# A two-block transformer layer on one core: the last block's entry, with the gates' rows moved among the norm's tiles and the dense work of eight rounds dealt out unevenly

## The chip, the cores and the metric

The kernel runs on one core of a Trainium2 chip. TensorE (PE in the profile) multiplies matrices; VectorE (DVE), ScalarE (ACT) and GpSimd (POOL) do the rest; SyncE's queue (SP) carries the weights. Every engine works through its own list of instructions in order and waits on semaphores for the others. The metric is the time of one execution on the device in microseconds (us), lower is better.

## The reference, cut to what matters

512 tokens of 1024 channels pass a first block (banded attention, pooling, a gated feed-forward) and then a second, hybrid block. The change touches the beginning of the second block only:

```python
hn = rms_norm_2(x, w_norm)
proj = jnp.einsum("bsd,de->bse", hn, w_in.astype(f32))
q_a, k_a, v_a, z_a, b_a, a_a, q_b, k_b, v_b, z_b = jnp.split(proj, idx, axis=-1)
qkv = jax.nn.silu(causal_depthwise_conv(jnp.concatenate([q_a, k_a, v_a], -1), conv_w.astype(f32)))
...
beta = jnp.transpose(jax.nn.sigmoid(b_a), (0, 2, 1))
g = -jnp.exp(a_log.astype(f32)) * jax.nn.softplus(a_a + dt_bias.astype(f32))
g = jnp.transpose(g, (0, 2, 1))
o_a = gated_delta_rule_chunked(q_a, k_a, v_a, g, beta)
```

`b_a` and `a_a` are the gates: 4 heads each, so 8 of the projection's columns. `rms_norm_2` needs one factor per token, the inverse root of the mean of squares over the 1024 channels. The projection is computed on the vector that is not yet multiplied by this factor, and the factor is applied when the product is read. So the products may begin before the factor is known, but no product can be read before it.

## The kernel before, in words

**Units.** Activations lie with channels on the 128 partitions: `X` is 8 tiles (`KT`) of 128 channels by 512 tokens. All weights come as units of 128 output channels by 1024 input channels. A unit is loaded into one of four slots (`RING`) of `raw`, rounded by ScalarE to `Wh`, and VectorE writes the rest `Wl = raw - Wh` (`split`). Activations are split the same way in `Hh` and `Hl`. A unit's product takes 8 steps of three 128x512 matmuls (Wh with Hh, Wh with Hl, Wl with Hh: L514, L515, L517), accumulated in one PSUM bank, and a ninth step without a matmul.

**The entry of the last block.** `post_tiles` adds the first block's output to `X` tile by tile. For each tile ScalarE writes `Hh` (L1711) and the squares `up_squares` (L1715), VectorE writes `Hl` (L1043). TensorE follows in `units_together` with turn 2: units c0 and c1 of head 0 together, per tile six products (L549) and four matmuls of the squares with a column of ones (L568, each in two passes). The last of these gives the column sums "cols". VectorE turns them into means (`rstd`, L1058), GpSimd raises them to the power -1/2 (L2097), and TensorE spreads these factors into a row over all partitions with four transposes (`norm_row`, L585). VectorE copies the row to `RB` (L1063), which every read of a product (L1068) multiplies with.

**The rounds.** Then `second_block` runs in rounds. One call `st(p)` advances each chain by one step (to its next `yield`) and then does p steps of the dense units in their order: c2, z0, z1, Kr, Qb, v of this head, then c0, c1, c2 of the next. All engines replay the same rounds, each with its own part of the chains. In stage 0 the first chain is `gate_chain`, which takes eight rounds: on TensorE 24 matmuls of the gates' weights `ba_h`, `ba_l` (8 output columns, L733 to L735) in round 1, four transposes of the gates' rows (L742) at the start of round 3, and two small products of `glog` (the cumulated and the summed log decay, "sums", L751 and L752) in round 7. `PACE_SCALARS = 3` gives each round three dense steps.

**VectorE's side.** After `RB` come the reads of c0 and c1 and their convolution taps (L1579, on `C3`, read `C` in the profile), one tap per unit and round, ahead of the chain's step in each round; the split of the next unit (L1029); in round 2 the copy of the gates' rows from PSUM to `tmp` (`gate_rows`, L1323); and further on the short operations that lead to `glog` (L1327 to L1352). The TensorE transposes L742 wait for that copy, and L751 waits for `glog`.

**Banks.** `bank_of` gives each product its PSUM bank, the second block's units 0 and 1 in turn. A product begins (`group_begins`) only when the product before it in that bank was read, so c2 in bank 0 waits for the read of c0.

**Later stages.** `prep` (head by head), `scan` and `diff` follow in the same rounds; the scan's first products are L898. L759 (`row_of`), the first of `prep`, spreads `gcum`.

Of the kernel before, what the change touches and what calls it, by code (L numbers as in the profile page):

```python
# [21 lines left out]
KT = D // P  # L22
# [56 lines left out]
OUT_LATE = [(k, r) for k in range(KT) for r in (GH - 1, 2 * GH - 1)]  # L79


PACE_SCALARS, PACE_END = 3, 1.5
PACE_SCORES, PACE_PREP = (None, 1.9, 1.9, 1.25), (1.5, 1.7, 1.7, 0.8)


# [64 lines left out]
def program(nc, ctx, x_in, w_units, w_ba, cols_in, mats_in, rope_in, rows_in, relb_in, counts_in,  # L150
# [142 lines left out]
    bank_of = {g: g % 2 for g in range(G_OUT + 2 * KT)}  # L293
    bank_of.update({2: 6, 3: 7})
    bank_of.update({G_UP + j: UP_BANKS[j % 6] for j in range(N_UP)})

    def group_before(g):

# [183 lines left out]
    def second_block(rounds_of, first, chains_of, unit_of):  # L482

        for a, b in STAGES:
            st = rounds_of(a, b)
            st.scanning = st.scoring = b is not None
            st.dense = [unit_of(st, a, n) for n in ("c2", "z0", "z1", "Kr", "Qb", "v")[a > 0:]]
            if a + 1 < GH:
                st.dense += [unit_of(st, a + 1, n) for n in ("c0", "c1", "c2")]
            if b is None:  # L490
                st.chains.append(first(st))
                while st.chains:
                    st(PACE_SCALARS)
            st.chains = chains_of(st, a, b)
            while st.scoring:
                st(PACE_SCORES[a])
            while st.chains:
                st(PACE_PREP[a])
            st.fill(1000)
# [3 lines left out]
    def tensor_program():  # L503
# [18 lines left out]
        def group_begins(g):  # L522

            before = group_before(g)
            if before is not None:
                pe.wait_ge(*sum_read(before))
            return PS[:, bank_of[g], :]
# [14 lines left out]
        def units_together(n0, g0, lags, turn, squares=None):  # L542


            banks = [group_begins(g0 + u) for u in range(len(lags))]

            def product(u, k, w, h, **ends):
                s, own = (n0 + u) % RING, slice(k * P, (k + 1) * P)
                return pe.matmul(banks[u], w[:, s, own], h[:, k, :], **ends)  # L549
            for m in range(KT + max(lags)):  # L550
                now = [(u, m - lag) for u, lag in enumerate(lags) if 0 <= m - lag < KT]
                if m < KT:
                    pe.wait_ge(*norm_hh.at(turn, m))
                for u, k in now:
                    weights_ready(n0 + u, k)
                    product(u, k, Wh, Hh, start=k == 0, stop=False)
                    product(u, k, Wl, Hh, start=False, stop=False)
                if m < KT:
                    pe.wait_ge(*norm_dv.at(turn, ("hl", m)))
                for u, k in now:  # L560
                    ins = product(u, k, Wh, Hl, start=False, stop=k == KT - 1)
                    if k == KT - 1:
                        ins.then_inc(unit_used, 1)
                if squares is not None and m < KT:
                    pe.wait_ge(*norm_sq.at(turn, m))
                    for t in range(NT):

                        ins = pe.matmul(PS[:, 3, t:t + 1], squares[:, m, tok(t)], ones[:],  # L568
                                        start=m == 0 and t == 0, stop=m == KT - 1 and t == NT - 1,
                                        skip_group_check=True)  # L570
                    if m == KT - 1:
                        ins.then_inc(*norm_pe.tick(turn, "cols"))
# [8 lines left out]
        def norm_row(turn):  # L581

            pe.wait_ge(*norm_gp.at(turn, "rstd"))
            for t in range(NT):
                ins = pe.transpose(PS[:, 2, tok(t)], rstd[:, t:t + 1].to_broadcast([P, P]), ident[:])  # L585
            ins.then_inc(*norm_pe.tick(turn, "bcast"))
# [140 lines left out]


        def gate_chain(st):
            pe.wait_ge(*lam_dv.at(0, "ba_lo"))  # L730
            for k in range(KT):
                w = slice(2 * GH * k, 2 * GH * (k + 1))
                pe.matmul(PS[0:2 * GH, 4, :], ba_h[:, w], Hh[:, k, :], start=k == 0, stop=False)  # L733
                pe.matmul(PS[0:2 * GH, 4, :], ba_h[:, w], Hl[:, k, :], start=False, stop=False)
                ins = pe.matmul(PS[0:2 * GH, 4, :], ba_l[:, w], Hh[:, k, :], start=False,  # L735
                                stop=k == KT - 1)
            ins.then_inc(*gate_pe.tick(0, "rows"))
            yield
            yield
            pe.wait_ge(*gate_dv.at(0, "rows"))  # L740
            for t in range(NT):
                ins = pe.transpose(PS[:, 5, 2 * GH * t:2 * GH * (t + 1)], gate_rows[:, tok(t)],  # L742
                                   ident[0:2 * GH, 0:2 * GH])
            ins.then_inc(*gate_pe.tick(0, "turned"))
            yield
            yield
            yield
            yield
            pe.wait_ge(consts_loaded, 48)
            pe.wait_ge(*gate_dv.at(0, "glog"))  # L750
            pe.matmul(PS[:, 4, 0:N16], mat(K_UPPER), flat(glog[:]), start=True, stop=True)  # L751
            pe.matmul(PS[:, 4, N16:2 * N16], ones[:].to_broadcast([P, P]), flat(glog[:]),  # L752
                      start=True, stop=True).then_inc(*gate_pe.tick(0, "sums"))
            yield

        def row_of(bank, columns):

            for t in range(NT):
                ins = pe.transpose(bank[:, tok(t)], columns[:, t:t + 1].to_broadcast([P, P]), ident[:])  # L759
            return ins  # L760
# [50 lines left out]
        def prep(st, i):  # L811
            yield
            pe.wait_ge(*gate_dv.at(0, "gcum"))
            if i:
                pe.wait_ge(*prep_ac.at(i - 1, "u"))
                pe.wait_ge(*prep_dv.at(i - 1, "wt"))
            row_of(b6, gcum[:, i, :]).then_inc(*prep_pe.tick(i, "g"))
            yield
            yield
            yield from idle(2)  # L820
            yield
            yield
            pe.wait_ge(*prep_ac.at(i, "sq"))
            for j in range(2):
                for t in range(NT):
                    ins = pe.matmul(b7[:, NT * j + t:NT * j + t + 1], sq[:, 1 - j, tok(t)], ones[:],
                                    start=True, stop=True)
            ins.then_inc(*prep_pe.tick(i, "sums"))
            yield
            pe.wait_ge(*prep_dv.at(i, "d"))  # L830
            pe.wait_ge(*decay_ac.at(i, "eg"))
            per_tile(b6, CK, CK).then_inc(*prep_pe.tick(i, "kk"))
            yield
            pe.wait_ge(*prep_dv.at(i, "ms"))
            turn_tiles(b7, CV).then_inc(*prep_pe.tick(i, "vt"))
            yield
            yield from idle(1 + (i in (0, GH - 1)))
            for lv in levels:
                pe.wait_ge(*prep_dv.at(i, ("t", lv - 1) if lv > 1 else "lm"))
                if lv == 1:  # L840
                    pe.wait_ge(*prep_ac.at(i, "strips"))
                    pe.wait_ge(*prep_dv.at(i, "lt"))
                if lv == KQ_LEVEL + 1:
                    pe.wait_ge(*prep_dv.at(i, "at"))
                if lv == 6:
                    pe.wait_ge(*prep_ac.at(i, "wide"))
                inverse_y(lv).then_inc(*prep_pe.tick(i, ("y", lv)))
                yield
                pe.wait_ge(*prep_ac.at(i, ("y", lv)))
                if lv == 1:  # L850
                    pe.wait_ge(*prep_dv.at(i, "vb"))
                inverse_t(lv).then_inc(*prep_pe.tick(i, ("t", lv)))
                yield
                if lv == KQ_LEVEL:
                    while st.scanning:
                        yield
                    turn_tiles(b6, CK).then_inc(*prep_pe.tick(i, "kt"))
                    pe.wait_ge(*prep_dv.at(i, ("t", lv)))
                    per_tile(b7, CK, CQ).then_inc(*prep_pe.tick(i, "qk"))
                    yield  # L860
                yield
            pe.wait_ge(*prep_dv.at(i, ("t", N_LEVELS - 1)))
            per_tile(b6, TiT, Vb).then_inc(*prep_pe.tick(i, "u"))
            per_tile(b7, Kb, TiT).then_inc(*prep_pe.tick(i, "w"))
            yield
# [108 lines left out]
            yield from unit_steps(st, name, unit(n, g))  # L974

        units_together(U_P2, G_P2, LAGS_LAST, 2, up_squares)
        norm_row(2)
        second_block(lambda a, b: Rounds(), gate_chain, chains_of, unit_of)


# [1364 lines left out]
```

## Time and profile before

| what | value |
|---|---|
| time, median of 3 runs | 1111.91 us (1110.41 to 1115.26) |
| profiled execution, its own time | 1109.57 us |
| its span | 1108.1 us |
| TensorE busy | 1062.4 us, 96% |
| VectorE busy | 646.0 us, 58% |
| ScalarE busy | 443.2 us, 40% |
| GpSimd busy | 89.5 us, 8% |
| mean granted TensorE clock | 0.989 of full speed |

Busy is what an engine works as a share of the span. The span is the profiled stretch, 1.5 us shorter than the execution's own time. "Idle before" beside an instruction is how long its engine had nothing to do before it, and "<-" names what ended that. The profile gives the granted clock as a share of full speed: 1.00 is 2.4 GHz and 0.50 is 1.2 GHz. Ends of matmuls are modelled and overlap the next one's start, so a matmul's cost in a dense stretch is the distance from start to start, and not the duration printed.

### The profile page before, as it was taken

What the parts mean: (1) busy time and instruction counts of PE and PEld (TensorE: products, weight loads), DVE (VectorE), ACT (ScalarE), POOL (GpSimd) and SP (SyncE); (2) the same over time, 40 slices, a digit from 0 to 9 for tenths busy, and PEclk for the clock granted to TensorE, in tenths of its full rate; (3) what the DMA queues carried; (4) which work ended last, traced back from release to release, by engine and by line L of the source; (5) the groups of instructions that cost most, each with busy time, mean ns of one, the idle gap of its engine ahead of it and who ended that gap; (6) DMA issues with size and microseconds to landing.
All of it is one profiled execution on the core that took longest, in us unless ns stands there. A gap on an engine that the chain in (4) does not pass through costs nothing.

```text
span 1108.1 us, 15316 instructions
## 1 busy us (share of the span) xinstructions
PE 1062.4 (96%) x6212; PEld 842.2 (76%) x6212; DVE 646.0 (58%) x1121; ACT 443.2 (40%) x773; POOL 89.5 (8%) x77
## 2 busy tenths in 40 slices
PE   7999999999999999999999999989989989988998
PEld 6777777778788888888888888867766866866776
DVE  6645454556437788777772122655576566466574
ACT  6233232344443544444442222443264254354531
POOL 1000000000210000000001000001120120120210
PEclk9999999999999999999999999999999989989999
DMA  8221313122321333333322233131111111110102
GB/s 333 84 83 57 95 58 95 58 77 78 112 95 57 96 114 97 113 96 95 95 95 88 103 114 114 36 95 58 58 39 54 62 39 39 59 56 21 58 20 76
DMA packets 25429, 90.72 MB, mean 82 GB/s; under 512 B 2880, under 2 KB 3136, under 8 KB 25232
## 3 DMA queue, kind: packets, MB, share of 16 engines
q1 hardware_dynamic: 23328, 83.90, 24.0%
q0 software_dynamic: 592, 3.54, 0.8%
q10 hardware_dynamic: 1440, 2.31, 0.6%
q8 instruction: 49, 0.80, 0.3%
q14 instruction: 20, 0.16, 0.0%
HBM read 87.64 MB, written 2.10 MB: 81 GB/s over the span
## 4 chain that ended last, share of the span: by engine, by line
PE 88%; DVE 7%; ACT 3%; issue 2%; POOL 0%; DMA 0%; ACTq 0%; DVEq 0%; POOLq 0%
PE PS L514 23%; PE PS L517 22%; PE PS L515 22%; PE PS L549 5%; PE PS L640 1%; DVE Wl L1029 1%; PE PS L769 1%; PE PS L1002 1%; PE PS L999 1%; PE PS L1000 1%; PE PS L653 1%; PE PS L946 1%; DVE C L1579 1%; ACT Wh L1697 1%; PE PS L663 1%
## 5 line engine op out<-in xcount | busy, mean ns | idle before, releaser
L514 PE MATMUL PS<-Hh,Wh 128*128 128x512 f32 x856 | 353.0, 412 | 0.6 <-ACT M L1817 0.6
L517 PE MATMUL PS<-Hh,Wl 128*128 128x512 f32 x856 | 336.1, 393 | 0.0
L515 PE MATMUL PS<-Hl,Wh 128*128 128x512 f32 x856 | 336.0, 392 | 0.0
L1029 DVE TENSOR_TENSOR Wl<-raw,Wh 128x1024 fp32r<-128x1024 f32 x155 | 188.9, 1224 | 193.9 <-ACT Wh L1697 192.1
L514 PEld LDWEIGHTS PS<-Hh,Wh 128*128 128x128 f32 x856 | 162.2, 189 | 44.4 <-issue 11.5
L1697 ACT ACTIVATE Wh<-raw 128x1024 fp32r<-128x1024 f32 x155 | 161.4, 1051 | 71.8 <-PE PS L517 60.9
L517 PEld LDWEIGHTS PS<-Hh,Wl 128*128 128x128 f32 x856 | 161.9, 189 | 35.2
L515 PEld LDWEIGHTS PS<-Hl,Wh 128*128 128x128 f32 x856 | 162.7, 190 | 31.6 <-issue 2.2
L514 PE MATMUL PS<-Ah,Wh 128*128 128x512 f32 x176 | 69.8, 396 | 0.0
L515 PE MATMUL PS<-Al,Wh 128*128 128x512 f32 x176 | 69.8, 396 | 0.0
L517 PE MATMUL PS<-Ah,Wl 128*128 128x512 f32 x176 | 69.8, 396 | 0.0
L1816 ACT ACTIVATE sq<-PS 128x512 f32<-128x512 f32 x16 | 9.6, 598 | 88.8 <-PE PS L517 88.8
L1068 DVE TENSOR_TENSOR tmp<-PS,RB 128x512 f32<-128x512 f32 x44 | 30.3, 692 | 21.0 <-PE PS L517 18.8
L1844 ACT ACTIVATE conv<-conv 128x512 f32<-128x512 f32 x22 | 13.9, 632 | 71.0 <-DVE conv L1271 71.0
L2107 POOL MEMSET ssum<- 128x512 f32 x2 | 1.1, 528 | 481.5 <-DVE Hl L1256 255.6
L517 PEld LDWEIGHTS PS<-Ah,Wl 128*128 128x128 f32 x176 | 33.1, 188 | 8.1
L515 PEld LDWEIGHTS PS<-Al,Wh 128*128 128x128 f32 x176 | 33.1, 188 | 8.1
L514 PEld LDWEIGHTS PS<-Ah,Wh 128*128 128x128 f32 x176 | 33.1, 188 | 8.1
L549 PE MATMUL PS<-Hh,Wh 128*128 128x512 f32 x72 | 30.1, 419 | 7.6 <-DVE Wl L1134 7.3
L1831 ACT ACTIVATE conv<-tmp,cols 128x512 f32<-128x512 f32 x44 | 35.2, 802 | 5.5 <-DVE tmp L1068 5.5
L1768 ACT ACTIVATE sq<-sq,nmax 128x512 f32<-128x512 f32 (+3 forms) x32 | 17.7, 554 | 44.3 <-DVE nmax L1194 43.7
L1271 DVE SCALAR_TENSOR_TENSOR conv<-tmp,cols,conv 128x510 f32<-128x510 f32 x44 | 33.0, 750 | 1.6
(310 smaller groups left out, 1479.0 us busy)
## 6 DMA issues: line engine op xcount, KB each, us to landing
raw<-in_w_units SPq DMA_DIRECT2D x155, 512.0 KB, 3.5
relb<-in_rel POOLq DMA_DIRECT2D x1, 2048.0 KB, 9.4
out<-X ACTq DMA_DIRECT2D x8, 256.0 KB, 2.1
X<-in_x SPq DMA_DIRECT2D x3, 512.0 KB, 7.4
X<-in_x SPq DMA_DIRECT2D x2, 256.0 KB, 4.3
raw<-in_w_units SPq DMA_DIRECT2D x2, 256.0 KB, 4.6
rope<-in_rope POOLq DMA_DIRECT2D x1, 512.0 KB, 4.0
mats<-in_mats POOLq DMA_DIRECT2D x1, 384.0 KB, 3.4
```

The source lines that it names most:

```text
L514: pe.matmul(bank, Wh[:, s, w], rhs[0](r), start=first and j == 0, stop=False)
L515: pe.matmul(bank, Wh[:, s, w], rhs[1](r), start=False, stop=False)
L517: ins = pe.matmul(bank, Wl[:, s, w], rhs[0](r), start=False, stop=last and end)
L549: return pe.matmul(banks[u], w[:, s, own], h[:, k, :], **ends)
L640: pe.matmul(PS[:, 2 + a, 0:nk], Q2[r, tok(qt)], K2[r, 0:nk], start=True, stop=True).then_inc(*att_pe.tick(i, ("scores", n, a)))
L1029: dv.tensor_tensor(Wl[:, s, :], raw[:, s, :], Wh[:, s, :].bitcast(F32), sub).then_inc(unit_split, 1)
L1068: return dv.tensor_tensor(dst, PS[:, bank_of[g], :], RB[:], mult).then_inc(bank_read[g % 2], 1)
L1271: dv.scalar_tensor_tensor(out=c[:, 2:], in0=y[:, 0:S - 2], scalar=col(C_CONV + 4 * j), in1=c[:, 2:], op0=mult, op1=add).then_inc(up_taps, 1)
L1697: ac.activation(Wh[:, s, :], raw[:, s, :], ACT.Copy).then_inc(unit_rounded, 1)
L1768: ac.activation(w, w, ACT.Exp, bias=nmax[:, b + a:b + a + 1], scale=1.0, accum_out=rsum[:, b + a:b + a + 1]).then_inc(*att_ac.tick(i, ("ex ...
L1831: ac.activation(conv[:, p % 2, j % 2, :], tmp[:, j % 2, :], ACT.Identity, bias=col(C_CONV + 4 * j + 3), scale=col(C_CONV + 4 * j + 2)).the ...
L1844: ac.activation(c, c, ACT.Gelu_apprx_tanh).then_inc(up_gelu, 1)
```

## The change

Four edits, all at the entry of the last block. The 24 gate matmuls leave `gate_chain` and stand in `units_together` at turn 2, three per tile, behind the tile's products. `norm_row(2)` leaves the place ahead of the rounds and becomes TensorE's part of the gate chain's second step, so the first dense steps, those of unit c2, come ahead of it. To allow that, c2 of head 0 goes to PSUM bank 6, and `prep` of head 0 waits for c2's read before it writes that bank. The eight rounds get 4, 2, 3, 3, 4, 5, 2 and 1 dense steps where each had 3, 24 in both cases.

```diff
-PACE_SCALARS, PACE_END = 3, 1.5
+PACE_GATES, PACE_END = (4, 2, 3, 3, 4, 5, 2, 1), 1.5
...
+    bank_of[G_P2 + 2] = 6
...
-                while st.chains:
-                    st(PACE_SCALARS)
+                for pace in PACE_GATES:
+                    st(pace)
+                assert not st.chains
...
             banks = [group_begins(g0 + u) for u in range(len(lags))]
+            if turn == 2:
+                pe.wait_ge(*lam_dv.at(0, "ba_lo"))
...
                     product(u, k, Wl, Hh, start=False, stop=False)
+                if turn == 2 and m < KT:
+                    w = slice(2 * GH * m, 2 * GH * (m + 1))
+                    pe.matmul(PS[0:2 * GH, 4, :], ba_h[:, w], Hh[:, m, :], start=m == 0, stop=False)
+                    pe.matmul(PS[0:2 * GH, 4, :], ba_l[:, w], Hh[:, m, :], start=False, stop=False)
                 if m < KT:
                     pe.wait_ge(*norm_dv.at(turn, ("hl", m)))
+                if turn == 2 and m < KT:
+                    ins = pe.matmul(PS[0:2 * GH, 4, :], ba_h[:, w], Hl[:, m, :], start=False,
+                                    stop=m == KT - 1)
+                    if m == KT - 1:
+                        ins.then_inc(*gate_pe.tick(0, "rows"))
...
         def gate_chain(st):
-            pe.wait_ge(*lam_dv.at(0, "ba_lo"))
-            for k in range(KT):
-                w = slice(2 * GH * k, 2 * GH * (k + 1))
-                pe.matmul(PS[0:2 * GH, 4, :], ba_h[:, w], Hh[:, k, :], start=k == 0, stop=False)
-                pe.matmul(PS[0:2 * GH, 4, :], ba_h[:, w], Hl[:, k, :], start=False, stop=False)
-                ins = pe.matmul(PS[0:2 * GH, 4, :], ba_l[:, w], Hh[:, k, :], start=False,
-                                stop=k == KT - 1)
-            ins.then_inc(*gate_pe.tick(0, "rows"))
-            yield
+            yield
+            norm_row(2)
             yield
             pe.wait_ge(*gate_dv.at(0, "rows"))
...
                 pe.wait_ge(*prep_dv.at(i - 1, "wt"))
+            else:
+                pe.wait_ge(*sum_read(G_P2 + 2))
             row_of(b6, gcum[:, i, :]).then_inc(*prep_pe.tick(i, "g"))
...
         units_together(U_P2, G_P2, LAGS_LAST, 2, up_squares)
-        norm_row(2)
         second_block(lambda a, b: Rounds(), gate_chain, chains_of, unit_of)
```

TensorE at the end of the norm's tiles, before the change: the last tile's `Hl` products, the squares' sums, the factors' row, and then the gates' matmuls.

```order
L549 MATMUL PS<-Hl,Wh 128x512 x2
L568 MATMUL PS<-ones,up_squares 128x1 x4
L585 MATMUL PS<-ident,rstd 128x128 x4
L733 MATMUL PS<-Hh,ba_h 8x512
L734 MATMUL PS<-Hl,ba_h 8x512
L735 MATMUL PS<-Hh,ba_l 8x512
```

The same place in the changed kernel (its lines are numbered anew: L553 was L549, L581 was L568, L516 to L519 were L514 to L517).

```order
L564 MATMUL PS<-Hh,ba_h 8x512
L565 MATMUL PS<-Hh,ba_l 8x512
L569 MATMUL PS<-Hl,ba_h 8x512
L553 MATMUL PS<-Hl,Wh 128x512 x2
L581 MATMUL PS<-ones,up_squares 128x1 x4
L516 MATMUL PS<-Hh,Wh 128x512
L517 MATMUL PS<-Hl,Wh 128x512
L519 MATMUL PS<-Hh,Wl 128x512
```

Three gate matmuls now stand in each of the eight tiles ahead of the squares' sums, and c2's first step follows the last sums directly.

TensorE around the transposes of the gates' rows (`ident,tmp`) in the changed kernel. Before the change, all 24 gate matmuls and six steps of c2 stood between the factors' row (`ident,rstd`) and these transposes.

```order
L598 MATMUL PS<-ident,rstd 128x128 x4
L516 MATMUL PS<-Hh,Wh 128x512
L517 MATMUL PS<-Hl,Wh 128x512
L519 MATMUL PS<-Hh,Wl 128x512
L516 MATMUL PS<-Hh,Wh 128x512
L517 MATMUL PS<-Hl,Wh 128x512
L519 MATMUL PS<-Hh,Wl 128x512
L748 MATMUL PS<-ident,tmp 128x8 x4
```

Two steps of c2 are left between the two; four stand ahead of the factors' row. Further on, 13 steps with matmuls stand between the transposes and the products of `glog`, where there were 10.

VectorE has the same instructions in the same order in both kernels. In the changed one they read as follows from the copy of the factors' row to the copy of the gates' rows.

```order
L1070 COPY RB<-PS 128x512
L1075 TENSOR_TENSOR Yc<-PS,RB 128x512 x2
L1586 SCALAR_TENSOR_TENSOR C_134<-Yc,cols,C_134 128x511 x2
L1036 TENSOR_TENSOR Wl<-raw,Wh 128x1024
L1586 SCALAR_TENSOR_TENSOR C_134<-Yc,cols,C_134 128x510 x2
L1330 COPY tmp<-PS 8x512
```

Nothing moved here: two reads, four taps and a split still stand between the two copies. ScalarE, GpSimd and SyncE keep their order too.

## Rows read from the trace of the kernel before

**Rows 1.** Timeline, TensorE, 717 to 730: start, duration, engine, line, operation, [idle before].

```profile
717.43 0.48 PE L549 MATMUL PS<-Hh,Wh 128*128 128x512 f32 x1
...
719.71 0.48 PE L549 MATMUL PS<-Hh,Wh 128*128 128x512 f32 x1
...
721.18 0.95 PE L568 MATMUL PS<-ones,up_squares 128*128 128x1 f32 x8
723.47 0.65 PE L585 MATMUL PS<-ident,rstd 128*128 128x128 f32 x4 [1.34 <-POOL rstd L2097]
723.88 0.48 PE L733 MATMUL PS<-Hh,ba_h 128*8 128x512 f32 x1
...
729.51 0.39 PE L514 MATMUL PS<-Hh,Wh 128*128 128x512 f32 x1
```

**Rows 2.** Timeline, ScalarE, two tiles of the entry.

```profile
713.91 0.72 ACT L1711 ACTIVATE Hh<-X,cols 128x512 fp32r<-128x512 f32 x1 [0.75 <-DVE X L1077]
...
715.90 0.72 ACT L1711 ACTIVATE Hh<-X,cols 128x512 fp32r<-128x512 f32 x1 [0.74 <-DVE X L1077]
```

**Rows 3.** Timeline, VectorE, from the factors' row to the gates' rows.

```profile
724.16 0.69 DVE L1063 COPY RB<-PS 128x512 f32<-128x512 f32 x1 [1.83 <-PE PS L585]
...
730.40 0.67 DVE L1323 COPY tmp<-PS 8x512 f32<-8x512 f32 x1
```

**Rows 4.** Windows, VectorE: stretch, its length, busy (instructions), granted clock, DMA share, GB/s.

```profile
724.16:731.07 6.91, 6.53 (x10) 1.00 0.11 23
```

**Rows 5.** Timeline, TensorE, from the gates' transposes to the products of glog.

```profile
733.68 0.41 PE L742 MATMUL PS<-ident,tmp 8*128 8x8 f32 x4
734.02 0.50 PE L514 MATMUL PS<-Hh,Wh 128*128 128x512 f32 x1
...
740.77 0.39 PE L517 MATMUL PS<-Hh,Wl 128*128 128x512 f32 x1
743.42 0.37 PE L751 MATMUL PS<-glog,mats 128*128 128x16 f32 x2 [2.26 <-DVE glog L1352]
```

**Rows 6.** Timeline, VectorE: c2's read, the end of glog, and what follows it.

```profile
735.73 0.69 DVE L1068 TENSOR_TENSOR Yc<-PS,RB 128x512 f32<-128x512 f32 x1 [3.35 <-PE PS L517]
...
743.10 0.17 DVE L1352 TENSOR_SCALAR glog<-small 128x16 f32<-128x16 f32 x1
...
744.92 0.17 DVE L1357 COPY gcum<-PS 128x16 f32<-128x16 f32 x1
```

**Rows 7.** Timeline, TensorE: head 0's prep begins.

```profile
748.75 0.60 PE L759 MATMUL PS<-ident,gcum 128*128 128x128 f32 x4
749.10 0.48 PE L514 MATMUL PS<-Hh,Wh 128*128 128x512 f32 x1
```

**Rows 8.** Timeline, TensorE: the first and last of three long idle times.

```profile
809.54 0.49 PE L898 MATMUL PS<-head_VN,head_Kd 128*128 128x128 f32 x2 [3.94 <-DVE head_VN L1485]
...
978.84 0.58 PE L898 MATMUL PS<-head_VN,head_Kd 128*128 128x128 f32 x1 [4.64 <-DVE head_VN L1485]
```

**Rows 9.** Windows around these idle times and one shorter: PE, PEld, DVE, ACT, POOL, clock.

```profile
809.00:816.00 7.00, 6.46 (x24) 4.84 (x25) 5.40 (x10) 3.37 (x5) 4.27 (x3) 0.76 0.23 76
889.60:893.50 3.90, 0.00 (x0) 0.00 (x0) 2.10 (x4) 3.53 (x4) 0.00 (x0) 0.91 0.00 0
892.00:900.00 8.00, 6.47 (x17) 4.72 (x18) 6.38 (x11) 4.38 (x5) 4.03 (x3) 0.57 0.22 66
974.20:978.80 4.60, 0.00 (x0) 0.00 (x0) 2.10 (x4) 4.22 (x5) 0.00 (x0) 0.93 0.00 0
978.00:986.00 8.00, 7.16 (x21) 5.33 (x22) 5.81 (x11) 4.38 (x5) 4.03 (x3) 0.57 0.23 66
929.00:931.00 2.00, 0.00 (x0) 0.00 (x0) 1.86 (x8) 1.75 (x10) 0.00 (x0) 1.00 0.66 174
```

**Rows 10.** Timeline, TensorE at the low clock.

```profile
897.11 0.63 PE L515 MATMUL PS<-Hl,Wh 128*128 128x512 f32 x1
897.54 0.63 PE L517 MATMUL PS<-Hh,Wl 128*128 128x512 f32 x1
```

## What the change should do, worked out before it was run

> **What bounds the kernel now.** TensorE is busy 1062.4 of 1108.1 us, so I read its timeline first, and in it only the entry of the last block, where the change lies. In the norm's tiles TensorE sets the pace: one tile takes it 719.71 - 717.43 = 2.28 us from start to start [rows 1], while ScalarE, which VectorE's `X` releases, makes a new `Hh` every 715.90 - 713.91 = 1.99 us [rows 2]. Then the timeline shows two idle times of TensorE: 1.34 us ahead of the factors' row, ended by GpSimd's `rstd` [rows 1], and 2.26 us ahead of the products of `glog`, ended by VectorE [rows 5]. Next come VectorE's rows over the same time. From `RB` to the end of the gates' copy (724.16 to 731.07) it is busy 6.53 of 6.91 us [rows 3, 4]. This copy was done 2.6 us before TensorE came to the transposes at 733.68 [rows 5], so it costs nothing before. Last, the windows on the granted clock, since idle time here can cost more than itself.
>
> **The moved gate matmuls.** 24 of them, from 723.88 to 729.51, are 5.63 us, 0.235 each [rows 1]. The 8 output columns make them no cheaper. They leave the place behind the factors' row and come into a stretch that TensorE bounds: a tile becomes 2.28 + 0.70 = 2.98 us, further still from the 1.99 of the others. So nothing hides them and nothing is saved: about 5.5 us later sums, 5.6 us less behind them. Bounds for this piece: 0 on the one side, and -2.3 us (2.28 - 1.99, eight times) if all the slack of the other engines could be used on the other; I take 0, as TensorE's issue is back to back.
>
> **The factors' row behind four steps of c2.** The squares' last group starts at 721.18 and lasts 0.8 to the next start, so TensorE is free at 722.0; the row came at 723.47 [rows 1]: 1.5 us that c2's work now fills. That goes: -1.5. In the changed kernel the sums are done at 722.0 + 5.5 = 727.5, and c2 runs 12 matmuls. A dense matmul costs (740.77 - 734.02) / 29 = 0.233 [rows 5], so 2.8 us: the row starts at 730.3. The factors are ready 1.5 us behind the sums, at 729.0, so there is no wait, but the row comes 1.3 us later than it could.
>
> **The new wait.** VectorE's order did not change. It begins `RB` 0.69 us behind the row's start (723.47 to 724.16), now at 731.0, and ends the gates' copy 6.91 us later [rows 4], at 737.9; a TensorE instruction follows the end of its VectorE releaser by 743.42 - 743.27 = 0.15 us [rows 5, 6], so the transposes start at 738.05. TensorE has only the four row transposes (749.10 - 748.75 = 0.35 [rows 7]) and 6 matmuls (1.4 us) until then: it is there at 732.05. It stands 6.0 us. Queued behind are the rest of c2 (whose read VectorE waits for), z0 and z1, all ready. Before, 5.6 + 4.2 us of work covered the same 7 us. Bounds: if VectorE's copy waited for nothing but its own input, the stall would be 0; if all of 6.91 + 0.69 + 0.15 us but the 1.75 us of work stands, 6.0. I take 6.0.
>
> **The wait for glog.** It runs from the transposes: 733.68 to 735.73 gives c2's read, and to 743.27 the end of `glog` [rows 5, 6], 9.6 us in all, now 747.65, products at 747.8. TensorE has 0.34 + 39 x 0.233 = 9.4 us of work for this time and is there at 747.5. Of a wait of 743.42 - 741.0 = 2.4 us, 0.3 is left. At that point 9 more matmuls (2.1 us) are done than before, so the kernel stands at 747.8 - 743.42 - 2.1 = +2.3 us. The same sum by pieces: -1.5 + 6.0 - 2.1 = +2.4.
>
> **What is late next.** `gcum` ended 745.09 - 743.27 = 1.8 us behind `glog` [rows 6], now 749.45. `prep`'s first transposes come 0.45 us and 12 matmuls (2.8) behind the products, at 751.0 where they stood at 748.75 [rows 7]: still no wait. From there all engines follow TensorE, and I find nothing that takes the shift back. The bank for c2 and its new wait in `prep` cost nothing: c2's read is 8 us and more ahead of it.
>
> **The clock.** There are three long idle times further on, all ahead of L898: 3.94 us before 809.5, the same before 893.5, and 4.64 us before 978.8 [rows 8]. After each the granted clock went from full (2.4 GHz) to half (1.2 GHz). The mean of a window gives the length: 2 x (1 - 0.76) x 7.0 = 3.4 us at half, 2 x (1 - 0.57) x 8.0 = 6.9 in both others [rows 9]. In the second and third it fell before TensorE began again, 2 x (1 - 0.91) x 3.9 = 0.7 us before 893.5 and 2 x (1 - 0.93) x 4.6 = 0.6 us before 978.8, which is 3.2 to 4.0 us behind the idle time's start; in the first it fell after. It did not fall for the idle times of 2.26 [rows 5] and 2.0 us [rows 9]. A stand of 6 us is longer than any of the three, so I expect the fall inside it, at 735.3 to 736.1, and the return 6.9 us later, at 742.2 to 743.0: 4.2 to 5.0 us of work at half clock. A matmul then takes 897.54 - 897.11 = 0.43 us [rows 10] instead of 0.233 and 46% of the time is lost: 1.9 to 2.3, or 0 if it does not fall and 3.2 if all 6.9 us fell on work. I take 2.2, near the middle of those the rows give. TensorE is then at the products of `glog` at 749.7; `glog` itself, whose chain holds c2's last 6 matmuls and the transposes at half clock (+1.3), at 749.1. So TensorE is the later one, no wait is left, and the sum is 749.7 - 743.42 - 2.1 = +4.2 us.
>
> The Trainium skill speaks against this change in "TensorE: Matmul & The Clock Gate", section "HAM oscillation — how this bites in real kernels": a long wait of TensorE throttles it, and the cost is half of the throttled time. By that rule the 4.6 us at half clock would cost 2.3 us, by the rows 0.46 of it, 2.1 us. The trace agrees that long idle times are followed by the low clock (3.94 us and more).
>
> **The sum.** +4.2 on the profiled execution's 1109.57 us is 1113.8; on the median of the three runs, 1111.91, it is 1116.1. The profiled one lies 2.3 below that median and 0.8 below the fastest of them, so I forecast between the two, nearer to the median: 1115.5 us. About 0.5%, 5.6 us, is what a measurement of this kernel can tell from no change, so the likeliest case counts as no change, on its slow side.
>
> **Rivals.**
> First, the stand without the fall of the clock: +2.3, about 1113.6. For it: the clock fell once only after work had begun again, and the stand lies between dense stretches. Against: three of three idle times over 3.9 us had it.
> Second, not slower: no stand at the transposes, because VectorE's copy does not hold them. Its place is L742 in round 3, its price the 6.0 us and the fall of the clock, and it decides where the copy ends before 732.05. Both old gaps would then close: -1.5 - 2.1 = -3.6, about 1107.8. Against it: two reads, four taps and a split stand ahead of the copy, 6.5 us of pure work [rows 4].
> Third, slower by more than 0.5%: the same stand and fall, and one of the later low stretches, 3.4 us long before [rows 9], becomes one of 6.9 as its phase shifts, 3.5 x 0.46 = 1.6 more: +5.8, about 1117.5. For it: the same idle time gave both lengths.
> Fourth, the reverse of it: one of the two long stretches becomes short, -1.6: +2.6, about 1113.9.
>
> **Chances.** Forecast 0.50, with its own range 1113.5 to 1117; clock does not fall 0.12; no stand 0.06; later stretch longer 0.20; later stretch shorter 0.12. The range holds all but the no-stand case and the runs' own spread: 1111 to 1119.5. Slower by over 0.5%: the third rival and a tenth of the forecast's case, 0.25. Faster by over 0.5%: even the no-stand case gives 0.3% only and needs the later stretches' help, 0.03. The rest, 0.72, within.
>
> **What would show it.** The tiles' period in TensorE's timeline at 2.98 us; no idle time ahead of the factors' row; an idle time of about 5.8 us (6.0 less the last matmul's tail) ahead of the gates' transposes, released by VectorE's copy to `tmp`; the granted clock at 0.50 around it and c2's last matmuls 0.43 us apart; under 0.5 us ahead of the products of `glog`; and `prep`'s first transposes about 4 us later, at 753. An idle time below 3 us at those transposes would prove the forecast wrong, and so would a start of `RB` that is not tied to the row's transposes.

## The result, and the profile after

The changed kernel takes 1115.91 us (median of 6 runs, 1114.82 to 1116.93), the kernel before 1112.21 us (6 runs, 1110.41 to 1115.26). The ratio is 1.0033 with a 95% interval of 1.002 to 1.0046: 3.7 us slower, inside the 0.5% within which the forecast called it no change, and with the sign that it gave (+4.2 us). The profiled execution took 1116.46 us, its span is 1115.0 us. Two of the executions behind this document, one of the kernel before and one of "gate matmuls back, L898 filled", ran at a mean granted clock of 0.809 and 0.555 and took 1245 and 1754 us; the medians and ratios leave them out.

The timeline of the changed kernel's TensorE at the entry: start, duration, line, operation, and idle time before.

```profile
718.88 0.48 PE L553 MATMUL PS<-Hh,Wh 128*128 128x512 f32 x1
...
721.85 0.48 PE L553 MATMUL PS<-Hh,Wh 128*128 128x512 f32 x1
...
726.96 0.95 PE L581 MATMUL PS<-ones,up_squares 128*128 128x1 f32 x8
727.77 0.48 PE L516 MATMUL PS<-Hh,Wh 128*128 128x512 f32 x1
...
730.62 0.60 PE L598 MATMUL PS<-ident,rstd 128*128 128x128 f32 x4
...
738.21 0.59 PE L748 MATMUL PS<-ident,tmp 8*128 8x8 f32 x4 [5.60 <-DVE tmp L1330]
738.73 0.80 PE L516 MATMUL PS<-Hh,Wh 128*128 128x512 f32 x1
739.32 0.63 PE L517 MATMUL PS<-Hl,Wh 128*128 128x512 f32 x1
739.75 0.63 PE L519 MATMUL PS<-Hh,Wl 128*128 128x512 f32 x1
...
749.56 0.29 PE L757 MATMUL PS<-glog,mats 128*128 128x16 f32 x2
...
752.78 0.60 PE L765 MATMUL PS<-ident,gcum 128*128 128x128 f32 x4
```

A tile now takes 721.85 - 718.88 = 2.97 us where [rows 1] had 2.28. There is no idle time ahead of the factors' row (1.34 us in [rows 1]) and none ahead of the products of `glog` (2.26 us in [rows 5]). The new one is the 5.60 us ahead of the gates' transposes, ended by VectorE's copy to `tmp`. Behind it the matmuls stand 0.43 us apart: TensorE is at 1.2 GHz.

VectorE's timeline over the same time.

```profile
731.25 0.69 DVE L1070 COPY RB<-PS 128x512 f32<-128x512 f32 x1 [3.15 <-PE PS L598]
...
737.48 0.67 DVE L1330 COPY tmp<-PS 8x512 f32<-8x512 f32 x1
...
741.70 0.69 DVE L1075 TENSOR_TENSOR Yc<-PS,RB 128x512 f32<-128x512 f32 x1 [2.23 <-PE PS L519]
...
749.07 0.17 DVE L1359 TENSOR_SCALAR glog<-small 128x16 f32<-128x16 f32 x1
```

From `RB` to the end of the gates' copy it takes 738.15 - 731.25 = 6.90 us, as in [rows 3] (6.91).

Windows of the changed kernel: stretch, length, busy of PE, PEld, DVE, ACT, POOL, granted clock, DMA share, GB/s.

```profile
735.00:743.00 8.00, 4.79 (x15) 3.87 (x16) 5.14 (x7) 0.58 (x1) 0.00 (x0) 0.57 0.24 66
768.00:774.00 6.00, 5.49 (x107) 3.86 (x108) 2.35 (x5) 1.62 (x4) 0.00 (x0) 0.72 0.08 30
814.00:822.00 8.00, 6.94 (x19) 5.10 (x20) 5.90 (x11) 4.38 (x5) 4.02 (x3) 0.57 0.22 67
```

The first is the stand: 2 x (1 - 0.57) x 8 = 6.9 us at half clock. The other two are the later low stretches that this execution has and the profiled one of before has not, or shorter: 3.4 us near 770 (before: full clock) and 6.9 us near 815, where [rows 9] has 3.4. So these two profiled executions differ by 6.9 us of span, of which 3.6 us arise at the entry, 0.4 ahead of it (the first product of the tiles is at 704.04 instead of 703.65) and 2.9 behind it.

### The profile page after: what moved, and what is told of

Its sections match the earlier page's. It is cut to its first block, busy times and chain, and to the rows that moved or that the text cites. A ratio compares the mean times of both kernels' runs of the same rounds, so it can differ in the third digit from the quotient of the medians.

```text
span 1115.0 us, 15317 instructions
## 1 busy us (share of the span) xinstructions
PE 1066.3 (96%) x6212; PEld 844.0 (76%) x6212; DVE 646.0 (58%) x1121; ACT 443.1 (40%) x773; POOL 89.4 (8%) x77
## 4 chain that ended last, share of the span: by engine, by line
PE 87%; DVE 7%; ACT 3%; issue 2%; DMA 1%; POOL 0%; SPq 0%; ACTq 0%; DVEq 0%; POOLq 0%
PE PS L516 23%; PE PS L519 22%; PE PS L517 22%; PE PS L553 4%; DVE Wl L1036 1%; PE PS L653 1%; PE PS L775 1%; PE PS L1009 1%; PE PS L1006 1%; PE PS L1007 1%; PE PS L666 1%; DVE C L1586 1%; PE PS L954 1%; ACT Wh L1704 1%; PE PS L676 1%
## 5 line engine op out<-in xcount | busy, mean ns | idle before, releaser
L516 PE MATMUL PS<-Hh,Wh 128*128 128x512 f32 x856 | 354.7, 414 | 0.6 <-ACT M L1824 0.6
L517 PE MATMUL PS<-Hl,Wh 128*128 128x512 f32 x856 | 337.3, 394 | 0.0
L519 PE MATMUL PS<-Hh,Wl 128*128 128x512 f32 x856 | 337.3, 394 | 0.0
L516 PEld LDWEIGHTS PS<-Hh,Wh 128*128 128x128 f32 x856 | 163.1, 191 | 44.6 <-issue 11.8
L519 PEld LDWEIGHTS PS<-Hh,Wl 128*128 128x128 f32 x856 | 162.7, 190 | 35.7
L517 PEld LDWEIGHTS PS<-Hl,Wh 128*128 128x128 f32 x856 | 163.4, 191 | 31.7 <-issue 2.3
L516 PE MATMUL PS<-Ah,Wh 128*128 128x512 f32 x176 | 69.8, 396 | 0.0
L517 PE MATMUL PS<-Al,Wh 128*128 128x512 f32 x176 | 69.8, 396 | 0.0
L519 PE MATMUL PS<-Ah,Wl 128*128 128x512 f32 x176 | 69.8, 396 | 0.0
L519 PEld LDWEIGHTS PS<-Ah,Wl 128*128 128x128 f32 x176 | 33.2, 188 | 8.1
L517 PEld LDWEIGHTS PS<-Al,Wh 128*128 128x128 f32 x176 | 33.1, 188 | 8.1
L516 PEld LDWEIGHTS PS<-Ah,Wh 128*128 128x128 f32 x176 | 33.1, 188 | 8.1
L553 PE MATMUL PS<-Hh,Wh 128*128 128x512 f32 x72 | 30.3, 421 | 8.1 <-DVE Wl L1141 7.3
L2030 ACT ACTIVATE C<-Yc,cols 128x512 f32<-128x512 f32 x12 | 8.6, 722 | 65.6 <-DVE Yc L1075 65.6
```

Of the source, the lines that this page charges most:

```text
L516: pe.matmul(bank, Wh[:, s, w], rhs[0](r), start=first and j == 0, stop=False)
L517: pe.matmul(bank, Wh[:, s, w], rhs[1](r), start=False, stop=False)
L519: ins = pe.matmul(bank, Wl[:, s, w], rhs[0](r), start=False, stop=last and end)
```

## The experiments

Cover is the work that TensorE has while VectorE is on its way to what TensorE needs next; where the cover ends too early, TensorE stands idle. Theory A is the forecast's: VectorE's way from the factors' row to the gates' copy is no longer covered, TensorE stands, and its clock falls. Theory B is the rival from the tiles: making the stretch that TensorE bounds 5.6 us longer is what costs. To compare traces without the noise of later stretches, I use the entry's length: from the first product of the norm's tiles to `prep`'s first transposes (`ident,gcum`). It is 748.75 - 703.65 = 45.1 us before and 752.78 - 704.04 = 48.7 us after. Ratios are to the kernel before, run on the same chip in the same set of runs, with the 95% interval. The runs came in four sets, down to "gate matmuls back", to "row alone", to "gate matmuls back, L898 filled" and the last line; the kernel before took 1112.1, 1112.5, 1112.4 and 1111.9 us in them.

| run | median us | ratio | entry us |
|---|---|---|---|
| before | 1112.1 (29 runs) | | 45.1 |
| changed, again | 1115.28 | 1.0024 (1.0015 to 1.0033) | 49.8 |
| gates' copy first | 1115.11 | 1.0021 (1.001 to 1.0032) | 48.6 |
| stand filled | 1114.81 | 1.0017 (1.0005 to 1.0029) | 47.3 |
| gate matmuls back | 1107.54 | 0.9949 (0.9936 to 0.9962) | 41.6 |
| rounds alone | 1110.62 | 0.9984 (0.9973 to 0.9995) | 44.6 |
| tiles alone | 1115.98 | 1.0031 (1.0019 to 1.0042) | 49.2 |
| row alone | 1111.34 | 0.9991 (0.9982 to 1.0) | 45.3 |
| before, L898 filled | 1105.69 | 0.9941 (0.9925 to 0.9958) | 46.6 |
| changed, L898 filled | 1109.21 | 0.9966 (0.9951 to 0.9981) | 48.6 |
| changed, both filled | 1106.57 | 0.996 (0.9939 to 0.9981) | 47.2 |
| gate matmuls back, L898 filled | 1102.63 | 0.9913 (0.9887 to 0.9938) | none |
| the same again | 1100.25 | 0.9898 (0.9882 to 0.9915) | 41.7 |

**The changed kernel again.**

> The changed kernel once more, timed beside the others of this set. Theory A (the gates' matmuls no longer cover VectorE's way from the factors' row to the gates' copy, so TensorE stands 5.6 us at the gates' transposes and its clock falls): again +3 to +5 us on before. Theory B (the cost comes from the lengthened norm tiles, 8 x 0.7 us): the same time, so this run alone tells nothing; it is the scale for the others. The granted clock should again be 0.50 behind the transposes in its trace, and the later low stretches may be 3.4 or 6.9 us each.

2.7 us slower by the ratio, and the same stand; here the low clock began at 738.15, 0.4 us before TensorE started again, so about 6.4 us of it fell on work, 4.5 us in the first profiled execution of this kernel, and the entry is 1 us longer.

```profile
738.55 0.59 PE L748 MATMUL PS<-ident,tmp 8*128 8x8 f32 x4 [5.60 <-DVE tmp L1330]
```

**The gates' copy first.** On VectorE:

```diff
         norm_sums(2)
+        dv.wait_ge(*gate_pe.at(0, "rows"))
+        dv.tensor_copy(gate_rows, PS[0:2 * GH, 4, :]).then_inc(*gate_dv.tick(0, "rows"))
         norm_row(2)
```

and the same two lines taken out of the chain's second round.

> The changed kernel with VectorE's copy of the gates' rows moved ahead of its copy of the factors' row, into time in which it waits. Theory A: no stand at the transposes any more (0 instead of 5.6 us). But VectorE is busy from RB on, 7.6 us with reads, taps and a split, so it reads c2 at about 738.9 only, glog ends 7.5 us later at 746.4, and TensorE, there at 741.8, stands some 4.6 us at the products of glog: net +1.0 us on before without a fall of the clock, +2 to +3 with one. Theory B: as the changed kernel, +3.7. A simple reading (only the copy's place costs) would give -3.6.

As theory A had it, in place and size. TensorE's timeline:

```profile
733.51 0.41 PE L748 MATMUL PS<-ident,tmp 8*128 8x8 f32 x4
...
747.45 0.58 PE L757 MATMUL PS<-glog,mats 128*128 128x16 f32 x2 [4.45 <-DVE glog L1357]
```

and VectorE's:

```profile
732.22 0.69 DVE L1070 COPY RB<-PS 128x512 f32<-128x512 f32 x1 [2.52 <-PE PS L598]
...
739.77 0.68 DVE L1075 TENSOR_TENSOR Yc<-PS,RB 128x512 f32<-128x512 f32 x1
...
747.12 0.17 DVE L1357 TENSOR_SCALAR glog<-small 128x16 f32<-128x16 f32 x1
```

The transposes wait for nothing, and c2 is complete before 736. But VectorE reads it at 739.77, with no idle time before: it had been busy since `RB`. The stand has moved to the products of `glog`. What TensorE waits for is VectorE's backlog behind the row, and not one copy.

**The stand filled.** On TensorE, ahead of the wait for the rows' copy:

```diff
             yield
+            keep_awake(11)
             pe.wait_ge(*gate_dv.at(0, "rows"))
```

> The changed kernel with 11 idle-time matmuls (identity by cols, into a bank that nobody reads) ahead of the wait at the gates' transposes, about 4.7 us of TensorE work with no use. Theory A: the transposes start at the same time (about 738.2), about 1 us of stand is left, the granted clock stays at 1.00 there, and the time is about 2 us under the changed kernel: +2.3 on before, not +3.7 to +4.2. Theory B: no difference to the changed kernel. If the clock were all of the loss: equal to before.

The trace (timeline, then a window):

```profile
738.82 0.41 PE L749 MATMUL PS<-ident,tmp 8*128 8x8 f32 x4 [0.85 <-DVE tmp L1331]
```

```profile
737.00:746.00 9.00, 8.15 (x39) 6.48 (x38) 7.21 (x15) 3.17 (x4) 0.00 (x0) 1.00 0.25 66
```

The clock stays at full, and the entry is 2.2 us longer than before, against 3.6 to 4.7 us in the changed kernel: the stand without its clock, as forecast (+2.3). In the times, though, it is not told from the changed kernel (1.0017 and 1.0024, intervals overlap). In its profiled execution a low stretch of 3.4 us came at 769, which the repeated changed kernel had not. So this run settles the mechanism at the entry, but not the gain in time.

**The gate matmuls back behind the row**, with the row behind three steps of c2, bank 6 and uneven rounds kept:

```diff
-PACE_GATES, PACE_END = (4, 2, 3, 3, 4, 5, 2, 1), 1.5
+PACE_GATES, PACE_END = (3, 3, 3, 3, 4, 5, 2, 1), 1.5
...
             yield
             norm_row(2)
+            for k in range(KT):
+                ...
+            ins.then_inc(*gate_pe.tick(0, "rows"))
             yield
```

The three gate matmuls per tile are taken out again (not shown).

> The factors' row behind three steps of c2 (bank 6 kept), the 24 gate matmuls back behind the row, rounds of 3, 3, 3, 3, 4, 5, 2, 1 steps. Theory A: the row starts at about 724.1 without a wait, 5.6 + 2.1 us of work cover VectorE's 7.6 us, no stand at the transposes, 0.3 us at glog: -1.5 - 2.1 = -3.6 us on before, about 0.9968. Theory B: also a gain, of the same size, since the tiles are short again; it differs from A in the runs where only one edit is made.

The timeline of its TensorE:

```profile
725.46 0.60 PE L589 MATMUL PS<-ident,rstd 128*128 128x128 f32 x4
...
733.58 0.41 PE L746 MATMUL PS<-ident,tmp 8*128 8x8 f32 x4
...
743.32 0.36 PE L755 MATMUL PS<-glog,mats 128*128 128x16 f32 x2 [0.22 <-DVE glog L1357]
```

No wait ahead of the row and the transposes, 0.22 us ahead of `glog`. The entry is 45.1 - 41.6 = 3.5 us shorter (expected 3.6). The time fell by more: 5.7 us by the ratio (4.2 to 7.1), 4.6 by the medians. Of what is above 3.5 us, 1.4 goes with the clock: its mean is 0.9875 over these 6 runs and 0.9861 over the 29 of before, 2 x 0.0014 x 1107 = 3 us less at half clock, 46% of it lost. Which stretches these are, the traces of single executions cannot say.

**The rounds alone.**

```diff
-PACE_SCALARS, PACE_END = 3, 1.5
+PACE_GATES, PACE_END = (3, 3, 3, 3, 4, 5, 2, 1), 1.5
```

> The kernel before with rounds of 3, 3, 3, 3, 4, 5, 2, 1 dense steps in place of eight times 3, nothing else. Theory A: three more steps of z1 stand ahead of the products of glog, the wait of 2.3 us there falls to 0.3, the rest is unchanged: -2.1 us. Theory B says nothing of it. If the wait comes back later (at prep's first transposes or at the sums of squares), 0.

```profile
724.89 1.11 PE L585 MATMUL PS<-ident,rstd 128*128 128x128 f32 x4 [1.34 <-POOL rstd L2097]
746.40 0.37 PE L751 MATMUL PS<-glog,mats 128*128 128x16 f32 x2 [0.22 <-DVE glog L1352]
```

The wait of 2.26 us became 0.22, and it did not come back: 1.8 us less by the ratio (2.1 expected). In this execution the clock was at half for 3.4 us from the row on (its 1.11 us are twice the usual), which is 1.6 us of its entry's 44.6.

**The tiles alone**: only the 24 matmuls moved into the tiles.

> The kernel before with only the 24 gate matmuls moved into the norm's tiles; the factors' row ahead of c2, c2 in bank 0, rounds of 3. Theory A: the cover between row and transposes falls from 9.8 to 4.2 us against 7.4 needed, a stand of about 3.1 us at the transposes beside the 1.3 and 2.3 us that stay: +3.1 us on before, up to +4.5 if the clock falls for a stand of that length. Theory B (the tiles' longer time is lost): +5.5 us and no stand.

```profile
729.99 1.06 PE L596 MATMUL PS<-ident,rstd 128*128 128x128 f32 x4 [1.34 <-POOL rstd L2100]
732.56 0.80 PE L514 MATMUL PS<-Hh,Wh 128*128 128x512 f32 x1 [1.51 <-DVE Yc L1071]
738.89 0.41 PE L745 MATMUL PS<-ident,tmp 8*128 8x8 f32 x4
748.62 0.37 PE L754 MATMUL PS<-glog,mats 128*128 128x16 f32 x2 [2.26 <-DVE glog L1355]
```

The total is theory A's (+3.5 us by the ratio, entry +4.1), and theory B's 5.5 us is out. My place was wrong in part: with the gate matmuls gone and c2 in bank 0, c2 must wait 1.51 us for c0's read, and the low clock (from 730.1 to 736.9) stretches its six steps so far that the rest of the wait is covered. Bank 6 takes this wait for c0's read away. The clock fell here directly behind the idle time of 1.34 us, which passed at full clock in the kernel before.

**The row alone**: `norm_row(2)` in the chain behind three steps of c2, bank 6, gate matmuls behind it, rounds of 3.

> The kernel before with only the factors' row moved behind three steps of c2 (c2 in bank 6, prep waiting for its read), the gate matmuls behind the row as before, rounds of 3. Theory A: the wait of 1.3 us ahead of the row goes, VectorE has the row 0.6 us later, 8.0 us of work still cover its 7.6 us: -1.5 us. Together with the run of the pace alone it should give the kernel with both, -3.6. A rival: VectorE is what sets this stretch, and the later row takes back 0.6 of it, -0.9.

```profile
724.33 0.60 PE L589 MATMUL PS<-ident,rstd 128*128 128x128 f32 x4
732.45 0.41 PE L746 MATMUL PS<-ident,tmp 8*128 8x8 f32 x4
742.18 0.37 PE L755 MATMUL PS<-glog,mats 128*128 128x16 f32 x2 [2.26 <-DVE glog L1357]
```

The wait ahead of the row is gone, nothing took its place. The products of `glog` begin 742.18 - 703.78 = 38.4 us behind the tiles' start, 39.8 before: 1.4 us earlier. By the ratio 1.0 us, with an interval from 0 to 2.

The three parts alone add up to 3.5 - 1.0 - 1.8 = +0.7 us, and the whole change costs 2.7 to 3.7 us. The difference is that two of them draw on the same cover: the six steps of c2 between row and transposes (4.2 us) stay with the tiles alone, but in the changed kernel four of them stand ahead of the row, and 1.4 us are left.

**Filling ahead of L898.** To see what the clock alone costs, 14 matmuls of 128 columns into a bank that is free there, in the three scans that overlap a `prep`:

```diff
+                if c == 0 and i < GH - 1:
+                    keep_awake_scan(14)
                 pe.wait_ge(*scan_dv.at(i, ("v", c)))
```

> The kernel before with the same filling ahead of L898, nothing else. Theory A: -6 us on before. It is the base for the two changed kernels with the filling, in which the later low stretches no longer blur the entry's own cost.

Windows of before with filling, around the three places:

```profile
806.00:816.00 10.00, 9.19 (x59) 7.55 (x58) 6.63 (x10) 5.78 (x6) 1.73 (x2) 1.00 0.15 56
889.00:899.00 10.00, 9.19 (x60) 7.83 (x59) 6.61 (x11) 6.25 (x7) 2.25 (x2) 1.00 0.17 52
972.00:982.00 10.00, 8.48 (x56) 7.20 (x55) 6.61 (x10) 6.37 (x7) 2.52 (x3) 1.00 0.18 52
```

All at full clock, where [rows 9] has 0.76 and 0.57, and 6.6 us less (6 expected), with not one instruction of use added. Low stretches of 3.4 us elsewhere remain and differ between the two executions: the one of before has them near 326 and 1022, this one at 700.6, 724.5 and 768.9.

> The changed kernel with the filling ahead of L898 only. Theory A: against the kernel before with the same filling +2.3 (the stand) and +2 (its low clock), +4.2 us in all; if the +3.7 us of the change came from later low stretches, they would now be near 0.

Against before with the same filling: 1109.21 - 1105.69 = +3.5 us (4.2 expected). The change's loss stays when the low stretches at L898 are gone, so they are not its cause. How much of the 3.5 us is the entry's, this pair does not show. The two entries differ by 48.6 - 46.6 = 2.0 us only, since that of before with filling has a low stretch of its own at 724.5, behind the idle time of 1.34 us; and the changed kernel's execution has two more of 3.4 us behind the entry, at 956.6 and 1021.4.

> The changed kernel with both fillings, ahead of L898 and ahead of the gates' transposes (11 matmuls of 256 columns). Theory A: the clock no longer falls at the stand, so about 2 us less than with the filling ahead of L898 alone, +2.3 on the kernel before with that filling. Theory that the clock at the stand costs nothing: no difference between the two.

A further 2.6 us less by the medians (2 expected), but only 0.7 by the ratios, 0.9966 and 0.996, whose intervals overlap: the gain in time stays open. Against before with the filling of L898 it is +0.9 us by the medians and +2.1 by the ratios (2.3 expected). What is shown is the clock and the entry: the mean granted clock over the twelve runs of each rose from 0.9919 to 0.9948, 2 x 0.0029 x 1108 = 6.4 us less at half clock, and in the traces the entry fell from 48.6 to 47.2 us, by the same 1.4 as with the stand filled alone (48.7 to 47.3). The same window in both traces, first with L898 filled only, then with both:

```profile
734.00:742.00 8.00, 4.84 (x15) 3.95 (x16) 5.12 (x7) 0.62 (x1) 0.00 (x0) 0.57 0.21 66
```

```profile
734.00:742.00 8.00, 7.15 (x35) 5.74 (x34) 6.19 (x10) 1.99 (x4) 0.00 (x0) 1.00 0.20 68
```

**The best of the parts together**: gate matmuls back, uneven rounds, L898 filled.

> The kernel with the gate matmuls back behind the row and the uneven rounds, and 14 idle-time matmuls of 128 columns (into b7, which nobody reads there) ahead of the first L898 of the three scans that overlap a prep, where TensorE stands 3.9 to 4.6 us. Theory A (a stand of that length makes the clock fall, and the low stretch costs 46% of the work in it): the three low stretches go, -1.6 - 2.9 - 2.9 as the trace of before has them, so about 6 us under the 1107.5 of the same kernel without filling. Rival: the fall comes from the small matmuls around, or the filling itself does not count; then no gain, or a loss of up to 1 us from filling that runs over.

The ratio is 0.9913, the median 1102.63 us, 4.9 us under the 1107.5 of the same kernel without filling (about 6 expected). The same kernel once more, for a trace:

> The kernel with the gate matmuls back behind the row, the uneven rounds and the filling ahead of L898 once more, for its trace. If the gain of the entry (-3.5 us of work) and that of the filling (-6.6 us on before) add up, 1112.2 - 10.1 = 1102 us; the low stretches at L898 gone, L898 waiting under 1.5 us, and the spread of its times set by what low stretches are left (at the entry and near 770), 1099 to 1106.

1100.25 us, 0.9898, the fastest kernel here. The two gains add up: 11.3 us less by the ratio, with an interval from 9.5 to 13.1 (10.1 expected). The waits of its TensorE: line waited for, total us, times, longest.

```profile
PE PS L777 <- DVE head_Ti L1436: 4.2, 2, 2.1
PE PS L910 <- DVE head_VN L1496: 3.4, 4, 1.5
PE PS L964 <- DVE head_Wd L1574: 3.3, 3, 1.3
```

Here L910 was L898: 3.4 us in four waits, 12.8 in the changed kernel, the rest being filled.

## Why the prediction was right, step by step

**The moved matmuls gain nothing.** Right: a tile takes 2.97 us (2.98 forecast), all of it on TensorE's path.

**The row behind four steps of c2.** Right: no wait; the row began at 730.62 (730.3 forecast; in this execution the tiles began 0.4 us later). The part alone was worth 1.0 us by the ratio and 1.4 in the trace (1.5 forecast).

**The new wait.** Right: transposes at 738.21 (738.05), idle time 5.60 us (5.8). The lever was the cover: 5.6 us of gate matmuls and 2.8 us of c2's steps went from between the row and the transposes to ahead of the row, and VectorE's 6.9 us there did not shrink. Moving the gate matmuls back, with three steps of c2 ahead of the row in place of four, turned +3 us into -5. Moving VectorE's copy instead only moved the stand, since its reads and taps still came between `RB` and c2's read.

**The wait for glog.** Right: gone in the changed kernel, products at 749.56 (749.7), and by itself worth 1.8 us (2.1).

**The clock.** Right in the mechanism: it fell inside the stand, near 735.9 (735.3 to 736.1 forecast), and rose near 742.7 (742.2 to 743.0). The filled stand showed its size at the entry, 1.4 us (3.6 less 2.2) in the profiled executions and 2.5 us (4.7 less 2.2) in the repetition. The forecast's sums with and without it are 4.2 - 2.3 = 1.9 us apart: 2.2 us of loss, of which 0.3 falls into the wait for `glog`. The rule of the Trainium skill ("TensorE: Matmul & The Clock Gate", section "HAM oscillation — how this bites in real kernels"), half of the throttled time, would be 3.4 us for all of the 6.9 us. The trace decides: TensorE had work in only 4.5 us of the 6.9 in the changed kernel's execution, the rest passed in the stand itself, and at 0.43 us a matmul instead of 0.233 that part costs 2.1 us.

**The sum.** +4.2 forecast for the entry, +3.6 in the profiled execution: `prep`'s transposes are 4.0 us later (752.78 against 748.75), but 0.4 of that came ahead of the entry. The medians have +3.7, the repetition +2.7 by its ratio. The forecast of the time, 1115.5, came out at 1115.91. That it is so close is in part luck: it adds 4.2 us to a base of 1111.3, chosen between the profiled execution and a median of three runs; the base was 1112.21, 0.9 us more, and the change 0.5 us less.

**What was not in it.** I took it that all behind the entry only follows. The order does, but not the clock: from one execution to the next the later stands of about 4 us are followed by 3.4 or by 6.9 us at half clock, and near 770 by 3.4 or none. I had this as a rival at 1.6 us; the profiled pair shows it at nearly twice that, 2.9 us behind the entry. Over many runs it does not add to the changed kernel's loss, rather the reverse: the mean granted clock is 0.9844 over the repetition's runs and 0.9861 over those of before, 2 x 0.0017 x 1114 = 3.8 us more at half clock, where the stand alone brings 6.9, and the time is 2.7 us longer for entries that were 3.6 and 4.7 us longer in the traces. Why fewer low stretches come elsewhere in it, and in the kernel with the gate matmuls back, stays open. The forecast also looked for low stretches behind long idle times only; the trace of before has two others (see the last section).

## What to carry to other kernels

Work that stands between a producer's last step and the point where its consumer must answer is a cover; before moving it forward, add up what the other engine does in order between the two, and leave at least that much. A wait that ends "early enough" in the trace before (2.6 us of slack here) is spent by 5.6 us of moved work even if no instruction was added. And where TensorE must stand for about 4 us or more, a few matmuls of no use ahead of the wait can be worth more than the edit one is working on: here 6.6 us for 42 of them ahead of L898. Ahead of the entry's stand they kept the clock up too, but the gain in time there could not be told from the spread of the runs.

## What the runs showed of the hardware

- In every trace without filling, the three stands of 3.9 to 4.6 us at L898 were followed by half clock, and so were the stands of 5.6 and 4.45 us at the entry. The idle times of 1.3 to 2.3 us were not settled: that of 2.26 us ahead of `glog` passed at full clock before, and with the row alone moved it was followed by 3.4 us at half (the first window below: 2 x (1 - 0.72) x 6). That of 1.34 us ahead of the factors' row passed at full clock before, was followed by 3.4 us at half with the rounds alone changed, and by 6.9 us with the tiles alone (second window: 2 x (1 - 0.62) x 9). With filling that left at most 1.5 us of idle at L898, no low stretch came there.
- A long stand is not the only place where the clock fell. The kernel before was at half clock for 3.4 us from 1022.5 on (third window: 2 x (1 - 0.57) x 4), where the longest idle times in the 12 us ahead were 1.31 and 1.22 us, and for as long near 326.
- The low stretches at the stands came as 3.4 or 6.9 us. In the changed kernel the fall came 2.3 us before TensorE began again (735.9 and 738.2) and it was 6.9 us; in the repetition it came 0.4 us before (738.15 and 738.55) and was 6.9 again; with the rounds alone changed it came 0.4 us before L898 (895.5 and 895.96) and was 3.4. What decides between the two lengths stays open.
- A 128x512 matmul with 8 output columns takes TensorE as long as one with 128: 0.235 us from start to start against 0.233.

The row alone moved, a window behind its products of `glog`; the tiles alone, a window around the factors' row; the kernel before, a window from 1022:

```profile
742.00:748.00 6.00, 5.82 (x21) 4.74 (x22) 2.02 (x5) 5.49 (x9) 0.00 (x0) 0.72 0.29 90
```

```profile
729.00:738.00 9.00, 6.50 (x19) 5.01 (x20) 6.54 (x10) 2.28 (x3) 1.69 (x4) 0.62 0.07 27
```

```profile
1022.00:1026.00 4.00, 4.00 (x42) 3.28 (x43) 2.26 (x5) 1.40 (x3) 0.00 (x0) 0.57 0.06 12
```
